# Attention maxima as four spare contraction rows, one chunk's low half on GpSimd, last output chunk consumed one piece later

## The reference, cut to what matters

```python
q = _rmsnorm(...); k = _rmsnorm(...)             # per head
c = cumsum(log_sigmoid(gate))                    # per head and token
s = q k^T * scale + c[t] - c[s];  causal mask
p = softmax(s);  o = p v;  h = h + o @ w_out     # layer 0
...                                              # MLP, then layer 1:
p = softmax(q k^T * scale + bias, sink);  h = h + (p v) @ w_out
```

## Time and profile before

| | us |
|---|---|
| median of 3 runs (1178.35 to 1182.67) | 1179.17 |
| profiled execution | 1181.87 |
| its span, first to last instruction | 1180.0 |
| PE busy | 1146.6 (97%) |
| POOL busy | 711.3 (60%) |
| DVE busy | 863.4 (73%) |
| ACT busy | 611.5 (52%) |
| mean granted clock of TensorE, share of 2.4 GHz | 0.991 |

### The profile page before, as it was taken

The page is one execution under the profiler, slowest core; times in us unless marked ns, Lnnn a source line. Parts: engine busy times, 40 slices in busy tenths (PEclk is TensorE's granted clock), DMA queues, the critical chain, the costliest instruction groups (busy, mean ns, idle before and its releaser), DMA issues.

```text
span 1180.0 us, 14620 instructions
## 1 busy us (share of the span) xinstructions
PE 1146.6 (97%) x5306; PEld 945.6 (80%) x5306; DVE 863.4 (73%) x957; ACT 611.5 (52%) x868; POOL 711.3 (60%) x477
## 2 busy tenths in 40 slices
PE   7999999998999999999999799998999999999998
PEld 6778878877888888888888488887888888888887
DVE  6677878866589667876865778886577768668764
ACT  3448788853444343434433678874364434444440
POOL 5523533534588878788873233334477887888781
PEclk9999999999999999999999899999999999999999
DMA  7221121122424332423043101111343323232221
GB/s 243 76 72 36 40 68 36 36 72 72 142 79 136 107 107 72 143 72 111 32 160 126 37 12 61 37 36 36 114 137 112 103 89 126 90 107 90 72 72 72
DMA packets 88497, 101.44 MB, mean 86 GB/s; under 512 B 3641, under 2 KB 68337, under 8 KB 88433
## 3 DMA queue, kind: packets, MB, share of 16 engines
q1 hardware_dynamic: 88224, 100.37, 26.2%
q10 hardware_dynamic: 208, 0.23, 0.1%
HBM read 98.47 MB, written 2.12 MB: 85 GB/s over the span
## 4 chain that ended last, share of the span: by engine, by line
PE 79%; issue 9%; POOL 6%; DVE 4%; ACT 2%; DMA 0%; POOLq 0%; DVEq 0%; ACTq 0%
PE ps L1642 23%; PE ps L1643 23%; PE ps L1644 23%; POOL w_lo L588 4%; PE ps L2121 2%; POOL fox_sq_lo L595 2%; DVE xn_lo L1154 1%; PE ps L1819 1%; ACT w_hi L688 1%; PE ps L2084 1%; PE ps L2103 0%; PE ps L2106 0%; PE ps L2105 0%; PE ps L2104 0%; DVE rst L1126 0%
## 5 line engine op out<-in xcount | busy, mean ns | idle before, releaser
L632 POOL TENSOR_TENSOR w_lo<-d_raw,w_hi 128x512 fp32r<-128x512 f32 x152 | 237.5, 1587 | 61.2 <-ACT w_hi L882 61.2
L1642 PE MATMUL ps<-xn_hi,w_hi 128*128 128x512 f32 x480 | 193.5, 403 | 1.7 <-DVE xn_lo L1154 1.7
L588 POOL TENSOR_TENSOR w_lo<-stage,w_hi 128x512 fp32r<-128x512 f32 x80 | 119.4, 1524 | 118.6 <-ACT w_hi L688 118.6
L1644 PE MATMUL ps<-xn_hi,w_lo 128*128 128x512 f32 x480 | 188.6, 393 | 0.0
L1643 PE MATMUL ps<-xn_lo,w_hi 128*128 128x512 f32 x480 | 188.3, 392 | 0.0
L882 ACT ACTIVATE w_hi<-d_raw 128x1024 fp32r<-128x1024 f32 x76 | 80.4, 1058 | 115.2 <-PE ps L1644 100.5
L1642 PE MATMUL ps<-w_hi,rows_hi 128*128 128x512 f32 x328 | 127.7, 389 | 0.0
L1643 PE MATMUL ps<-w_lo,rows_hi 128*128 128x512 f32 x328 | 127.6, 389 | 0.0
L1644 PE MATMUL ps<-w_hi,rows_lo 128*128 128x512 f32 x328 | 127.6, 389 | 0.0
L632 POOL TENSOR_TENSOR w_lo<-stage,w_hi 128x512 fp32r<-128x512 f32 x72 | 105.3, 1488 | 25.5 <-ACT w_hi L882 25.5
L632 POOL TENSOR_TENSOR ring_lo<-stage,ring_hi 128x512 fp32r<-128x512 f32 x56 | 88.0, 1601 | 42.1 <-ACT ring_hi L882 42.1
(11 more groups left out here) (258 smaller groups left out, 2727.9 us busy)
## 6 DMA issues: line engine op xcount, KB each, us to landing
stage<-in_w_up SPq DMA_DIRECT2D x32, 1024.0 KB, 5.3
d_raw<-in_w_down SPq DMA_DIRECT2D x64, 512.0 KB, 3.5
stage<-in_w_in_a SPq DMA_DIRECT2D x16, 512.0 KB, 4.5
stage<-in_w_out_a SPq DMA_DIRECT2D x4, 1024.0 KB, 4.9
stage<-in_w_q_b SPq DMA_DIRECT2D x4, 1024.0 KB, 4.9
stage<-in_w_out_b SPq DMA_DIRECT2D x4, 1024.0 KB, 4.8
stage<-in_w_in_a SPq DMA_DIRECT2D x3, 1024.0 KB, 5.7
x_in<-in_x SPq DMA_DIRECT2D x4, 512.0 KB, 5.5
```

The lines of the kernel that those rows point to most:

```text
L588: ins = nc.gpsimd.tensor_tensor(w_lo[:, s, c], stage[:, s, c], w_hi[:, s, c].bitcast(F32), ALU.subtract)
L632: ins = nc.gpsimd.tensor_tensor(lo[:, c], raw[:, c], hi[:, c].bitcast(F32), ALU.subtract)
L1642: mm(out_, st_hi, mv_hi, start=start, stop=False)
L1644: return mm(out_, st_lo, mv_hi, start=False, stop=stop)
```

## The change

1. Maxima. `diag`, its DVE operation and its matmuls go. DVE adds `nm` to a running `fox_shift` (128x4 for each head); one small matmul (`fox_turn`, 4 output rows, 128 columns) turns it; DVE spreads it block by block into four of the 64 other rows of `qk_hi` on the query side (4x512, from PSUM), which face ones on the key side. The next pair's maxima are then relative to the present shift, hence the running sum. `c` moves from rows 0 to 15 to rows 16 to 31 of the picked rows.
2. `fox_shift` lies at 77 KB of the operand area.
3. The low half of output chunks 0 to 5 of layer 0 moves from DVE to POOL, behind the squares t=1 of its step.
4. In both layers the piece with chunk 7 of the first output unit stands behind seven chunks of the second unit rather than four. In layer 0 the pieces ahead of the last pair's scores are cut otherwise.

```diff
+            V.tensor_scalar(fox_shift[:]..., ident[:, 0:2 * TB], 0.0, None, ALU.mult)
+            dve.wait_ge(constants_ready, 4)
+            V.memset(pick[0:TB, :], 1.0)
...
+            for e in range(2):
+                rows = slice(64 - 64 * e, 64 - 64 * e + TB)
+                ins = V.tensor_scalar(qk_hi[rows, 0, e, :]..., ctemp[rows, ...], 0.0, None, ALU.mult)
...
+            V.tensor_copy(c_split[0:TB, :], ct[0:TB, 3, :]).then_inc(gate_vector_step, 1)
...
             def fox_max(j):
                 for e in range(2):
                     dve.wait_ge(fox_max_scores_done, 2 * j + e + 1)
-                    after(dve, fox_diag_ready, 2 * j - 1 + e)
+                    after(dve, fox_shift_ready, 2 * j - 1 + e)
...
-                    after(dve, fox_scores_done, 2 * j - 1 + e)
-                    V.tensor_tensor(diag[:, e, :]..., ident[...], nm[...], ALU.mult).then_inc(fox_diag_ready, 1)
+                    V.tensor_tensor(fox_shift[:, e, :], fox_shift[:, e, :].bitcast(F32), nm[:, e, :], ALU.add
+                                    ).then_inc(fox_shift_ready, 1)
+                for e in range(2):
+                    dve.wait_ge(fox_shift_turned, 2 * j + e + 1)
+                    rows = slice(64 - 64 * e, 64 - 64 * e + TB)
+                    V.tensor_tensor(qk_hi[rows, 0, e, :]..., ps[0:TB, SCORE_BANKS[e][0], None, 0:P]...,
+                                    ident[0:TB, 0:TB, None]..., ALU.mult).then_inc(fox_rows_ready, 1)
...
                 fox_norm(i, 0)
-                if not (isinstance(i, int) and i < 2):
-                    out_lo(0, FILL_OUT_A, i - 2)
                 fox_norm(i, 1)
...
                 fox_squares(i, 1)
+                if not (isinstance(i, int) and i < 2):
+                    pool.wait_ge(xn_hi_ready, KC * FILL_OUT_A + i - 1)
+                    nc.gpsimd.tensor_tensor(one[2], one[0], one[1].bitcast(F32), ALU.subtract).then_inc(xn_ready, 1)
...
+                    if turn_before is not None and k == KC - 2:
+                        fox_turn(turn_before, 0)
...
+            def fox_turn(j, e):
+                pe.wait_ge(fox_shift_ready, 2 * j + e + 1)
+                mm(ps[0:TB, SCORE_BANKS[e][0], 0:P], fox_shift[:, e, :], ident_r[:], start=True, stop=True
+                   ).then_inc(fox_shift_turned, 1)
...
                 for e in range(2):
-                    pe.wait_ge(fox_diag_ready, 2 * j + e + 1)
+                    pe.wait_ge(fox_rows_ready, 2 * j + e + 1)
...
-                        mm(o, ones_r[:], diag[:, e, qs], start=False, stop=False)
...
-                proj_pair(i, s, 1, (i, 0))
+                proj_pair(i, s, 1, (i, 0), i - 1)
+                fox_turn(i - 1, 1)
                 fox_scores(i - 1)
...
-            out_piece(0, 0, both, range(0, 3))
+            out_piece(0, 0, both, range(0, 2))
             fox_max_scores(PAIRS - 1)
-            out_piece(0, 0, both, range(3, 6))
+            out_piece(0, 0, both, range(2, 5))
+            fox_turn(PAIRS - 1, 0)
+            out_piece(0, 0, both, range(5, 6))
+            fox_turn(PAIRS - 1, 1)
             fox_scores(PAIRS - 1)
             fox_pv(PAIRS - 1)
             out_piece(0, 0, both, range(6, 7))
-            out_piece(0, 1, both, range(0, 4))
+            out_piece(0, 1, both, range(0, 7))
             out_piece(0, 0, both, range(7, 8))
-            out_piece(0, 1, both, range(4, 8))
+            out_piece(0, 1, both, range(7, 8))
             proj_out_rest(0)
```

More of the change, by code:

```diff
@@ L262, in build @@
         pick = at("pick", [64, HEADS], F32, area + 76 * KB)
+        fox_shift = at("fox_shift", [P, 2, TB], F32R, area + 77 * KB)
         ct = at("ct", [P, 4, T], F32, area + 46 * KB)
-        diag = at("diag", [P, 2, T], F32R, area + 46 * KB)
         raw = at("raw", [P, 2, T], F32, area + 70 * KB)
@@ L351, in build @@
         fox_max_ready = sem("fox_max_ready")
-        fox_diag_ready = sem("fox_diag_ready")
+        fox_shift_ready = sem("fox_shift_ready")
+        fox_shift_turned = sem("fox_shift_turned")
+        fox_rows_ready = sem("fox_rows_ready")
         fox_scores_done = sem("fox_scores_done")
@@ L450, in build @@
         SCORE_BANKS = ((2, 3, 4), (5, 6, 7))
+        C_ROW = 16
         TURN_BANKS = (2, 3, 0, 1, 6, 3, 0, 7)
@@ L492, in _ @@
                     sp.wait_ge(wf_zero, 2)
-                    sp.dma_start(bf[0:HEADS, :], b_f[0].rearrange("(h o) -> h o", o=1)).then_inc(wf_landed, 16)
-                    sp.dma_start(wf[:, :, 0:HEADS], w_in[:, :, 3 * D:3 * D + HEADS]).then_inc(wf_landed, 16)
+                    sp.dma_start(bf[C_ROW:C_ROW + HEADS, :], b_f[0].rearrange("(h o) -> h o", o=1)).then_inc(wf_landed, 16)
+                    sp.dma_start(wf[:, :, C_ROW:C_ROW + HEADS], w_in[:, :, 3 * D:3 * D + HEADS]).then_inc(wf_landed, 16)
             def load_pair(i, s):
@@ L619, in fox_step @@
                 fox_squares(i, 1)
+                if not (isinstance(i, int) and i < 2):
+                    pool.wait_ge(xn_hi_ready, KC * FILL_OUT_A + i - 1)
+                    one = [t[:, bass.ds(i - 2, 1), :].rearrange("p a n -> p (a n)") for t in (o_t, o_hi[0], o_lo[0])]
+                    nc.gpsimd.tensor_tensor(one[2], one[0], one[1].bitcast(F32), ALU.subtract).then_inc(xn_ready, 1)
             fox_step(1, 0)
@@ L1211, in _ @@
                 V.tensor_copy(dst[:], src)
-            V.tensor_tensor(pick[:], ident[0:64, 0:HEADS], ident[0:64, 32:32 + HEADS], ALU.add)
+            V.tensor_tensor(pick[:], ident[0:64, C_ROW:C_ROW + HEADS], ident[0:64, 32 + C_ROW:32 + C_ROW + HEADS], ALU.add
+                            ).then_inc(constants_ready, 1)
+            V.tensor_scalar(fox_shift[:].rearrange("p e b -> p (e b)"), ident[:, 0:2 * TB], 0.0, None, ALU.mult)
+            dve.wait_ge(constants_ready, 4)
+            V.memset(pick[0:TB, :], 1.0)
             V.memset(vx[:, :, HD:2 * HD], 1.0).then_inc(ones_ready, 1)
@@ L1227, in _ @@
                                     ctemp[rows, None, C_ONES - C_TEMP:C_ONES - C_TEMP + P].to_broadcast([64, TB, P]))
+            ins.then_inc(ones_ready, 1)
+            dve.wait_ge(ones_ready, 2)
+            for e in range(2):
+                rows = slice(64 - 64 * e, 64 - 64 * e + TB)
+                ins = V.tensor_scalar(qk_hi[rows, 0, e, :].rearrange("p (b n) -> p b n", b=TB),
+                                      ctemp[rows, None, C_ONES - C_TEMP:C_ONES - C_TEMP + P].to_broadcast([TB, TB, P]),
+                                      0.0, None, ALU.mult)
             ins.then_inc(ones_ready, 1)
@@ L1243, in _ @@
             dve.wait_ge(gate_vector_step, 5)
+            V.tensor_copy(c_split[0:TB, :], ct[0:TB, 3, :]).then_inc(gate_vector_step, 1)
+            dve.wait_ge(gate_vector_step, 6)
             def fox_c(i):
@@ L1284, in fox_max @@
                     dve.wait_ge(fox_max_ready, 2 * j + e + 1)
-                    after(dve, fox_scores_done, 2 * j - 1 + e)
-                    V.tensor_tensor(diag[:, e, :].rearrange("p (b n) -> p b n", b=TB),
-                                    ident[:, None, :].to_broadcast([P, TB, P]),
-                                    nm[:, e, :, None].to_broadcast([P, TB, P]), ALU.mult).then_inc(fox_diag_ready, 1)
+                    V.tensor_tensor(fox_shift[:, e, :], fox_shift[:, e, :].bitcast(F32), nm[:, e, :], ALU.add
[3 more added lines that the diff above has]
+                    rows = slice(64 - 64 * e, 64 - 64 * e + TB)
+                    V.tensor_tensor(qk_hi[rows, 0, e, :].rearrange("p (b n) -> p b n", b=TB),
+                                    ps[0:TB, SCORE_BANKS[e][0], None, 0:P].to_broadcast([TB, TB, P]),
+                                    ident[0:TB, 0:TB, None].to_broadcast([TB, TB, P]), ALU.mult).then_inc(fox_rows_ready, 1)
             def reciprocal(y, den, refined, n):
@@ L1328, in _ @@
             fox_max(7)
+            dve.wait_ge(xn_ready, KC * FILL_OUT_A + KC - 2)
             out_lo(0, FILL_OUT_A, KC - 2)
@@ L1742, in _, with proj_pair @@
             pe.wait_ge(v_stored, TB)
-            def proj_pair(i, s, t, sum_before=None):
+            def proj_pair(i, s, t, sum_before=None, turn_before=None):
                 if t == 0:
@@ L1829, in fox_step @@
                     pe.wait_ge(v_stored, 2 * TB)
-                    pe.wait_ge(ones_ready, 2)
+                    pe.wait_ge(ones_ready, 3)
                 fox_max_scores(i - 1)
-                proj_pair(i, s, 1, (i, 0))
+                proj_pair(i, s, 1, (i, 0), i - 1)
+                fox_turn(i - 1, 1)
                 fox_scores(i - 1)
@@ L2160, in _ @@
             out_piece(1, 0, both, range(6, 7))
-            out_piece(1, 1, both, range(0, 4))
+            out_piece(1, 1, both, range(0, 7))
             out_piece(1, 0, both, range(7, 8))
-            out_piece(1, 1, both, range(4, 8))
+            out_piece(1, 1, both, range(7, 8))
             proj_out_rest(1)
```

## The result

| | us |
|---|---|
| before, median of 11 runs | 1181.42 |
| changed, median of 11 runs | 1187.24 |
| ratio, 95% interval | 1.0047 (1.0036 to 1.0058) |
| changed, span of the profiled execution (before: 1180.0) | 1184.9 |

The change costs 5.8 us by the ratio (4.3 to 6.9). The forecast was +7.4 us and 1186.6.

A forecast was written before the change was run, and what follows sets the result against it. PE was taken as 97% busy, with PE's and POOL's chains closing on each other in the attention. Terms -0.9 - 2.3 + 0.8 + 8.1 + 1.7 = +7.4 us on 1179.17 gave 1186.6, range 1181 to 1192.5.

The forecast's parts named there:

- step 1: First attention step, fox_sum(i, 1) to the next: PE, not held up by POOL, wins 1.1 - 0.2, so -0.9 us.
- steps 2 to 7: Later attention steps: three with POOL first cost +1.0, three with DVE first gain 3.3, so -2.3 us.
- last pair: Last pair's scores: head 0 also waits for head 1's maxima and held sums, +0.8 us, bounds -1.0 and +1.2.
- moved piece, both layers: Output projections: chunk 7 moved later delays w_lo for the third unit, +8.1 us, bounds 7.5 and 8.5.
- clock behind it: After the longer w_lo waits: clock stays low at least as long, 0 to +1.7 a layer, +1.7 us for both.
- Rival (d): Output projections: w_lo isn't set by unit 12's end, so the moved piece is free; -8 us, 1171.2, chance 0.05.
- the 1 us named as a sign: Attention steps: PE idle over 1 us, ended by DVE, ahead of L1802 or the turns would show the forecast right.
- The kind with DVE first: Attention steps where DVE precedes POOL: first sum free, second held to 18.05, scores end at 22.05; 22.15 us a step.
- Rival (a): Attention: sums into fox_shift are never held; +1.8 us, 1181.0, chance 0.15.
- Rival (b): Attention: sums are held, but DVE gets the first turn in all steps; +4.2 us, 1183.4, chance 0.17.
- (c): Attention: new waits over 1 us make the clock fall, POOL first in all steps; about +15 us, 1194, chance 0.13.
- Constants and the low half on POOL: Five small DVE operations before the first norms, and POOL's extra part behind the squares: both hidden, 0 us each.

The follow-up runs named there:

- the filler: The changed kernel with 30 unused matmuls of 512 columns in PE's wait for the third unit of either layer; ratio 1.0018 to the kernel before.
- the first experiment: The changed kernel with the output pieces of both layers back in the order of before; ratio 0.9981 to the kernel before.

## Why the prediction was right, and where it was off

The forecast of 1186.6 lies 0.6 us from the measured 1187.24, and that closeness is luck: the difference was forecast 1.6 too large, and the median of three runs from which it started, 1179.17, lay 2.2 below the 1181.42 of eleven. So what follows compares the difference, term by term.

Differences between the two profiled executions, taken between instructions that both have:

| term | forecast | in the profiles |
|---|---|---|
| until the first maxima's scores (87.24, now 87.70) | 0 | +0.5 |
| step 1 | -0.9 | -2.5 |
| steps 2 to 7 | -2.3 | -3.5 |
| last pair | +0.8 | +0.8 |
| moved piece, both layers | +8.1 | +7.9 |
| clock behind it | +1.7 | +0.2 |
| 650 to 803 us, same work in both | 0 | +1.5 |
| sum | +7.4 | +4.9 |

**The moved piece** was right in mechanism and size: +4.06 in layer 0, and in layer 1 (824.13 - 803.11) - (819.49 - 802.29) = +3.8. The two experiments on it measured 7.8 and 9.5 us. There was no wait for chunk 7 to hide; what moved was the end of the first unit's use. Rival (d) fell.

**The steps** were right in mechanism. Both kinds appeared, three of each, at 23.0 and 21.9 where I had worked out 23.1 and 22.15. The three of each were carried over, not worked out: POOL was first in steps 3 to 5 before and in 3, 5 and 6 now, and each step that changes its kind moves the sum by 1.1. PE's waits in the steps with POOL first, 0.38 and 0.58, together 0.96, lay just under the 1 us named as a sign. The kind with DVE first was sized 0.25 too long: I had POOL's squares end between S + 21.7 and 22.1 and took the upper part; in step 7 they ended at S + 21.8 (232.42 + 1.56 - 212.19), 0.06 ahead of `fox_sum`. So POOL is still what bounds these steps. Rival (a), the free sum, fell: median 0.86 us, up to 1.30, and the run with one SBUF input shows what it would have been. Rival (b) fell as well. Two of the rivals' sums had slips: (b)'s -5.5 is -5.25 by the steps' own figures, and (c) leaves out the -0.9 of step 1. Neither changes what fell.

**The last pair**: `fox_sum(7, 1)` to `fox_pv` took 256.89 - 234.04 = 22.85 us. Before it was 261.61 less the start in this row of PE's timeline before, 22.0:

```profile
239.59 0.51 PE L1764 MATMUL ps<-fox_sq_hi,blk_r 128*128 128x512 f32 x1 [0.38 <-POOL fox_sq_lo L595]
```

**The clock term** is the one mis-sized, and what lay beside it was held for constant. Behind the moved piece I had taken the middle of 0 and 1.7 a layer for a longer low stretch. In the profiles it stayed low 3.4 us behind PE's return in layer 0 and 4.2 in layer 1, against 3.4 in both before: +0.2 by the table. The forecast also held the rest of the clock for constant, and it isn't. Before, it had fallen once more in step 1, here it did not, and none of the other profiles has this fall, those with the old attention included. That is 1.7 of the 2.5 us there, by chance; the 0.8 that is left is near the 0.9 forecast (in the run with the low half on POOL alone, without the fall, the same stretch took 12.57 us, in the changed kernel 11.72). The busy time of the kernel before shows it:

```profile
90.00:91.00 1.00, 1.00 (x3) 0.72 (x3) 1.00 (x3) 1.00 (x1) 1.00 (x1) 0.50 0.00 0
```

And the changed kernel had a low stretch near 675 where the kernel before had none:

```profile
675.00:676.00 1.00, 1.00 (x3) 0.77 (x3) 0.00 (x0) 0.96 (x2) 0.00 (x0) 0.50 1.06 368
```

The clock alone doesn't explain the +1.5, though: from 650 to 680 us it was low for 10.2 us in either profile, only in other places. Ahead of this stretch PE had waited longer. Before and changed, the same operation on DVE beside POOL, and PE's wait behind it:

```profile
669.66 0.69 DVE L1133 SCALAR_TENSOR_TENSOR q_rst<-sqt,q_rst 128x512 f32<-128x512 f32 x1
673.36 1.13 PE L2064 MATMUL ps<-sqt,kept 128*128 128x512 f32 x2 [2.03 <-ACT sqt L998]
...
668.95 1.86 DVE L1141 SCALAR_TENSOR_TENSOR q_rst<-sqt,q_rst 128x512 f32<-128x512 f32 x1
673.79 1.18 PE L2099 MATMUL ps<-sqt,kept 128*128 128x512 f32 x2 [3.44 <-ACT sqt L1006]
```

The profiles with the low half on POOL alone and with the filler show the same: the operation took 1.84 and 1.86, PE waited 3.44 and a low stretch followed. In the other seven profiles it took 0.69 to 1.73 and PE waited 2.86 or less. One of the seven, that of the pieces moved alone, has a low stretch behind the place all the same, after a wait of 1.84. The long wait appears in one profile with the old attention and in two with the new, and is missing from others of both kinds, so it is not shown to come from the change.

This +1.5 and the 1.7 of step 1 nearly cancel, and that is luck. Rival (c), falls in the new waits of the attention, did not happen in any profile here.

**Constants and the low half on POOL** were costed at 0. The latter is shown by its own run; the constants lie in the first +0.5, which is also what the first loads differ by (a wait of 5.7 us before, 6.2 now, for the first DMA), so no cost of them is seen.

The difference by timing, 5.8, lies between the profiles' 4.9 and the forecast.

## What to carry to other kernels

Ahead of moving work behind a wait, look whether there is a wait, and follow what the moved instruction's end releases: here it freed a weight slot for a chain of 8 us through two engines, which no longer fit behind what was left. Time taken from an engine that is 97% busy is worth little (here 0.9 of 10 us) while another engine's result arrives 0.06 us ahead of its use; find it by reading who finished last before each join, not by the waits. Let a consumer start at the first quarter of a slow producer.

## What the runs showed of the hardware

A 128x4 operation on VectorE with both inputs in SBUF takes 0.16 us alone and up to 1.30 beside GpSimd, with one input in PSUM 0.16 in all 16 cases. Which of GpSimd and VectorE gets ahead moved whole steps by 1.1 us, and starts 0.01 us apart in the timeline went with either outcome (0.17 in step 4, 1.30 in step 6). In the run where the operation was free, all six steps took 21.88 to 21.90 us.

TensorE's granted clock after a wait of 3.1 us is not settled by the wait. Four kernels have it in both layers: it fell to 1.2 GHz in five of the eight cases (both of before and of the run without diagonal matmuls, layer 1 of the low half on POOL) and stayed at 2.4 GHz in three (both of the first experiment, layer 0 of the low half on POOL). It was then low behind PE's return for 3.0 to 3.5 us, once for 5.9. After 7.2 us it was low in all six cases without filler, for 3.4 to 4.9 us behind PE's return.
